# Part of the last expert's weights loaded early, first gather in four pieces, two chunks' keys interleaved at the start, in a hybrid decoder step

## The reference, cut to what matters

```python
m = rmsnorm(mem, g_mem); k = m @ w_k; v = m @ w_v                  # 256 memory tokens
x = x + mixer(rmsnorm(x, g_mix), ...)                              # w_in 1024x2560, w_out
x = x + cross_attn(rmsnorm(x, g_xattn), k, v, w_q, w_xo)           # 4 heads of 256; own cached k, v per sample
h = rmsnorm(x, g_moe)
top_logit, top_e = top_k(h @ w_router + b_router, 4)               # of 32 experts
gates = softmax(top_logit)
for each expert e:                                                 # tokens that chose e
    gate, up = split(x_e @ w1[e] + b1[e])                          # 1024 x 2048
    out_e = ((clip(up) + 1) * glu(min(gate, 7))) @ w2[e] + b2[e]   # 1024 x 1024
x = x + sum_e gate_e * out_e
y = rmsnorm(x, g_final)
```

## Time and profile before

| | |
|---|---|
| median of 3 runs | 1196.09 us (1193.36 to 1196.84) |
| the profiled execution | 1195.74 us |
| its span, first to last instruction | 1193.9 us |
| PE busy | 1157.0 us, 97% |
| DVE, ACT, POOL busy | 306.9, 157.7, 28.2 us |
| DMA | 458.34 MB, mean 384 GB/s |
| chain that ended last | PE 72%, DMA 25%, DVE 1%, ACT 1% |
| expert units of 2048 KB issued | 182, some 33 us from issue to landing |
| granted clock | 0.997 of full speed |

### The profile page before, as it was taken

One profiled execution on the slowest core, in us unless ns is written; L12 is line 12 of the kernel. 1 busy time (PEld: TensorE's weight loads), 2 busy tenths in 40 slices (PEclk: granted clock), 3 DMA queues, 4 the chain that ended last, 5 costly groups with the idle time before them and its releaser, 6 DMA issues.

```text
span 1193.9 us, 14908 instructions
## 1 busy us (share of the span) xinstructions
PE 1157.0 (97%) x5937; PEld 604.6 (51%) x5937; DVE 306.9 (26%) x638; ACT 157.7 (13%) x242; POOL 28.2 (2%) x63
## 2 busy tenths in 40 slices
PE   9999999999999999999999999999999999999997
PEld 8888888784434344444444343434343434343433
DVE  5124533332121212122222212121212121212124
ACT  2011011031101210121021011101110111010102
POOL 0000000000000000000000000000000000000000
PEclk9999999999999999999999999999999999999999
DMA  9963444998999999999999999999999999999995
GB/s 366 398 238 129 131 155 150 427 390 335 426 426 428 428 428 429 428 428 430 428 429 427 429 429 429 428 428 429 428 429 428 428 430 428 430 427 428 428 428 221
DMA packets 40398, 458.34 MB, mean 384 GB/s; under 512 B 6032, under 2 KB 6800, under 8 KB 8496
## 3 DMA queue, kind: packets, MB, share of 16 engines
q1 hardware_dynamic: 37440, 454.12, 90.7%
q10 hardware_dynamic: 2928, 3.80, 1.0%
HBM read 454.41 MB, written 3.23 MB: 383 GB/s over the span
## 4 chain that ended last, share of the span: by engine, by line
PE 72%; DMA 25%; DVE 1%; ACT 1%; issue 0%; SPq 0%; DVEq 0%; ACTq 0%
PE ps L1307 25%; PE ps L1084 15%; DMA ring<-in_w_dn 14%; PE ps L1425 13%; DMA arena<-in_w_dn 8%; PE ps L1281 7%; PE ps L1298 3%; DMA ring<-in_w_gu 3%; PE ps L1111 2%; PE ps L1318 2%; PE ps L1192 1%; DMA ring<-in_w_k 1%; PE ps L1177 1%; PE ps L1211 1%; PE ps L1167 1%; PE ps L1414 1%
## 5 line engine op out<-in xcount | busy, mean ns | idle before, releaser
L1307 PE MATMUL ps<-ring,arena 128*64 128x512 f32 x1536 | 349.9, 597 | 5.6 <-DMA ring<-in_w_gu 4.8
L1307 PEld LDWEIGHTS ps<-ring,arena 128*64 128x64 f32 x1536 | 103.1, 136 | 200.6 <-issue 184.7
L1084 PE MATMUL ps<-arena,ring 128*128 128x264 f32 (+1 forms) x800 | 178.9, 385 | 0.0
L1425 PE MATMUL ps<-ring,arena 128*64 128x512 f32 x736 | 165.4, 595 | 9.4 <-DMA ring<-in_w_dn 9.4
L1084 PEld LDWEIGHTS ps<-arena,ring 128*128 128x128 f32 x800 | 151.8, 190 | 25.3 <-issue 0.2
L1307 PE MATMUL ps<-arena 128*64 128x512 f32 x512 | 116.9, 598 | 2.8 <-DMA arena<-in_w_gu 2.4
L1020 DVE COPY arena<-ps 64x512 f32<-64x512 f32 x31 | 21.5, 694 | 369.1 <-PE ps L1425 369.1
L1425 PEld LDWEIGHTS ps<-ring,arena 128*64 128x64 f32 x736 | 52.7, 137 | 112.9 <-issue 106.8
L962 DVE TENSOR_TENSOR resid<-resid,ps 128x264 f32<-128x264 f32 x128 | 53.1, 429 | 173.3 <-PE ps L1298 172.8
L1281 PEld LDWEIGHTS ps<-arena 128*128 128x128 f32 x768 | 90.1, 195 | 14.8 <-issue 14.8
L1281 PE MATMUL ps<-arena 128*128 128x128 f32 x768 | 94.5, 280 | 1.8 <-ACT arena L626 1.8
(11 more groups left out here) (201 smaller groups left out, 504.4 us busy)
## 6 DMA issues: line engine op xcount, KB each, us to landing
ring<-in_w_gu SPq DMA_DIRECT2D x92, 2048.0 KB, 32.6
ring<-in_w_dn SPq DMA_DIRECT2D x44, 2048.0 KB, 32.9
arena<-in_w_gu SPq DMA_DIRECT2D x32, 2048.0 KB, 33.7
arena<-in_w_dn SPq DMA_DIRECT2D x14, 2048.0 KB, 32.8
ring<-in_w_in SPq DMA_DIRECT2D x10, 1024.0 KB, 27.5
ring<-in_kc SPq DMA_DIRECT2D x8, 1024.0 KB, 4.8
ring<-in_vc SPq DMA_DIRECT2D x8, 1024.0 KB, 5.1
ring<-in_w_gu SPq DMA_DIRECT2D x8, 1024.0 KB, 8.8
```

The costliest lines, as they stand in the source:

```text
L1084: last = mm(b[:, 0:width], w[:, k, P * (m % 2):P * (m % 2) + P], source(k), start=(k == 0), stop=(k == KT - 1))
L1307: last = mm(ps[64 * h:64 * h + 64, bank + n, :], tile[:, k, SLOTS * half:SLOTS * half + SLOTS], w[:, at:at + 512], start=(k == 0), stop=(k ...
L1425: last = mm(ps[64 * h:64 * h + 64, 4, :], hid[i % 2][:, k, :], w[:, at:at + 512], start=(k == 0), stop=(k == KT - 1))
```

## The change

Five edits stand in the diff.

1. **Start.** `FIRST_PARTS` has two parts left. After them comes the first half (k 0-3) of the second key chunk, then the second half of the memory, then the second halves of both key chunks. PE does m = 2, 3 for k 0-3 before m = 0 to 3 for k 4-7.
2. **Cross-attention.** DVE copies the probabilities of heads 0 and 1 before the sample softmax's reciprocal and scale. The copies have a semaphore of their own, `probs_copied`.
3. **Router and first gather.** The permutation moves from ACT's copies to the place where PE writes the transposes in PSUM: neighbouring columns of a transpose's output lie 128 floats apart. ACT reads and writes whole rows. `h_tok[2]` is not zeroed; the gather contracts over its 8 rows alone. The gather is issued quarter by quarter: only ga0 ahead of the first expert matmul, ga1 to ga3 in the middle of units 0, 1 and 2; the gates' transposes go to unit 3.
4. **Order in the experts' rounds.** For odd i: `gather_half` after u = 0, `turn_gate_up` after u = 1, `combine_two` after u = 2 and u = 3. In the last round but one the last expert's `turn_gate_up` goes into the down matmuls of expert 30, after two of their eight k.
5. **Stash.** The 1 MB row k = 7 of expert 31's gate and up is loaded to a buffer of its own in `arena` ahead of the kc chunks. Unit 3 of expert 31 then loads only its other 1 MB, and SP's step for it is split accordingly.

```diff
-FIRST_PARTS = [(0, 2), (2, 4), (4, 8)]
+FIRST_PARTS = [(0, 2), (2, 4)]
+ARENA = 23280
...
+        stash = view(stash_at, SLOT)
...
+            half = 256 * KT // 2
+            sp.dma_start(ring[:, 1, 0:half], w_k[1, :, 0:half]).then_inc(part_landed[2], 16)
+            sp.dma_start(mem_raw[:, KT // 2:, :], mem_t[:, KT // 2:, :]).then_inc(mem_in[2], 16)
+            for n in range(2):
+                sp.dma_start(ring[:, n, half:], w_k[n, :, half:]).then_inc(landed[n], 16)
...
+                if (kind, c) == ("kc", 0):
+                    rows = w_gu[NE - 1, KT - 2:KT].rearrange("k p n -> (k p) n")
+                    sp.dma_start(stash[:], rows.rearrange("(p j) n -> p (j n)", j=ROWS_GU)[:, SLOT:2 * SLOT]).then_inc(stash_in, 16)
...
+            last_step = turns * 4 + 2
+            unit_free(last_step, 3)
+            sp.dma_start(unit_buffer(n)[:, 0:SLOT],
+                         rows.rearrange("(p j) n -> p (j n)", j=ROWS_GU)[:, 0:SLOT]).then_inc(unit_landed[n], 16)
+            step(last_step, 2, NE - 2, NE - 1, range(4, UNITS))
...
-                by_row = h_tok[n // 2][0:rows, 512 * (n % 2):512 * (n % 2) + 512].rearrange(
-                    "t (b j p) -> t b p j", b=2, j=ROWS_GU)
-                nc.scalar.activation(by_row, bank(("htok", n))[0:rows].rearrange("t (b p j) -> t b p j", b=2, j=ROWS_GU),
+                nc.scalar.activation(h_tok[n // 2][0:rows, 512 * (n % 2):512 * (n % 2) + 512], bank(("htok", n))[0:rows],
                                      ACT.Copy, scale=rstd_tok[0:rows, n // 2:n // 2 + 1]).then_inc(tok_copied, 1)
...
+            for h in range(2):
+                copy_probs(h)
             dve.wait_ge(s_exp, 5)
             link(nc.vector.reciprocal(att_s[:, 8:9], att_s[:, 8:9]))
-            TS(s_s[:], s_s[:], att_s[:, 8:9], None, ALU.mult).then_inc(emptied, 1)
-            dve.wait_ge(kv_stored, 32)
-            for h in range(HEADS):
-                copy(probs_t[:, h, :, :], filled(("pT", h)).rearrange("p (m q) -> p m q", m=2)).then_inc(emptied, 1)
+            TS(s_s[:], s_s[:], att_s[:, 8:9], None, ALU.mult).then_inc(emptied, 1 + HEADS)
+            for h in range(2, HEADS):
+                copy_probs(h)
...
+            for m in range(2, 4):
+                keys(m, 0, KT // 2)
+            for m in range(4):
+                if m % 2 == 0:
+                    pe.wait_ge(landed[m // 2], 16)
+                keys(m, KT // 2, KT).then_inc(grp, 1)
...
-                    last = turn(b[0:width, P * f:P * f + P],
+                    pair = b[0:width, 2 * P * (f // 2):2 * P * (f // 2) + 2 * P]
+                    by_row = pair.rearrange("t (j h i) -> t h i j", j=ROWS_GU, h=2)[:, f % 2]
+                    last = turn(by_row,
                                 h_fm[:, 4 * (n % 2) + f, P * (n // 2):P * (n // 2) + width], ident[:])
...
-            gather(begin(("ga", 0)), 0, range(2), begun=True).then_inc(ga_filled, 1)
-            gather(begin(("ga", 1)), 0, range(2, 4)).then_inc(ga_filled, 1)
+            def gather_quarter(n):
+                return gather(begin(("ga", n)), n // 2, range(2 * (n % 2), 2 * (n % 2) + 2), begun=(n == 0))
+
+            gather_quarter(0).then_inc(ga_filled, 1)
...
+                pe.wait_ge(ga_copied, u + 1)
                 pe.wait_ge(unit_landed[u], 16)
                 halves = gate_up_unit(unit_buffer(u), u, xg[0], 0, FIRST_BANK)
                 next(halves).then_inc(half_used, 1)
-                if u == 1:
+                if u < 3:
+                    gather_quarter(u + 1).then_inc(ga_filled, 1)
+                else:
                     turn_gates()
...
+                            if i % 2:
+                                if u == 0:
+                                    gather_half()
+                                elif u == 1:
+                                    turn_gate_up(e)
+                                else:
+                                    combine_two(e, i, 2 * u - 4)
+                            elif u == 0:
                                 turn_gate_up(e)
...
-                    if early:
-                        turn_gate_up(e + 1)
...
+                            if early and k == 2:
+                                turn_gate_up(e + 1)
```

More of the change, by code:

```diff
@@ L234, in build @@
         unit_landed = [sem(f"unit_landed{n}") for n in range(RING_UNITS)]
-        part_landed = [sem(f"part_landed{n}") for n in range(2)]
+        part_landed = [sem(f"part_landed{n}") for n in range(3)]
         bias_split = sem("bias_split")
@@ L397, in unit_free, with step @@
                     sp.wait_ge(w_used, e * 4 + n - 2)
-            def step(e, i, expert, next_expert):
-                for n in range(UNITS):
+            def step(e, i, expert, next_expert, units=range(UNITS)):
+                for n in units:
                     unit_free(e, n)
@@ L436, in _ @@
             for i in range(3):
-                step(NE - 4 + i, i, NE - 4 + i, NE - 3 + i)
+                step(NE - 4 + i, i, NE - 4 + i, NE - 3 + i, range(UNITS if i < 2 else 3))
             sp.wait_ge(iters_ready, 2)
@@ L443, in _ @@
                 with sp.Fori(1, end >> 3) as again:
+                    step(again * NE - 2, 2, NE - 2, NE - 1, range(3, UNITS))
                     step(again * NE - 1, 3, NE - 1, 0)
@@ L448, in _ @@
                     for i in range(3):
-                        step(again * NE + NE - 4 + i, i, NE - 4 + i, NE - 3 + i)
+                        step(again * NE + NE - 4 + i, i, NE - 4 + i, NE - 3 + i, range(UNITS if i < 2 else 3))
+            last_step = turns * 4 + 2
+            unit_free(last_step, 3)
+            n = (STEP_AT[2] + 3) % RING_UNITS
+            rows = w_gu[NE - 1, KT - 2:KT].rearrange("k p n -> (k p) n")
+            sp.dma_start(unit_buffer(n)[:, 0:SLOT],
+                         rows.rearrange("(p j) n -> p (j n)", j=ROWS_GU)[:, 0:SLOT]).then_inc(unit_landed[n], 16)
+            step(last_step, 2, NE - 2, NE - 1, range(4, UNITS))
             for part, (k, k_end) in enumerate(LAST_PARTS):
@@ L656, in four_experts @@
                         pos = pos + 1
+                    if i % 2 and not final or i == 1:
+                        act.wait_ge(side_filled, pos + 2)
+                        copy_gathered(nxt, 1)
                     if not (final and i == 3):
@@ L1090, in _, with keys @@
             keep_busy(ps[:, 7, :], 9)
-            first_keys = ring[:, 0, :].rearrange("p (k n) -> p k n", k=KT)
+            first_keys = ring[:, 0:2, :].rearrange("p c (k n) -> p c k n", k=KT)
+            def keys(m, k_first, k_end):
+                for k in range(k_first, k_end):
+                    pe.wait_ge(mem_ready, k + 1)
+                    last = mm(bank(("k", m))[:, 0:NMEM], first_keys[:, m // 2, k, P * (m % 2):P * (m % 2) + P],
+                              mem[:, k, :], start=(k == 0), stop=(k == KT - 1))
+                return last
             for part, (k_first, k_end) in enumerate(FIRST_PARTS):
-                pe.wait_ge(landed[0] if part == 2 else part_landed[part], 16)
+                pe.wait_ge(part_landed[part], 16)
                 for m in range(2):
[L1095 to L1102, removed]
+                    keys(m, k_first, k_end)
+            pe.wait_ge(part_landed[2], 16)
+            for m in range(2, 4):
[4 more added lines that the diff above has]
+                keys(m, KT // 2, KT).then_inc(grp, 1)
                 if m == 2:
@@ L1105, in _ @@
                     sum_squares("mem_ssq", 1, NMEM, 2)
+            for m in range(4, KT):
+                project("w_k", m, lambda k: mem[:, k, :], "k")
             for c in range(4):
@@ L1280, in gather @@
                             pe.wait_ge(p_built if t == 2 else first_p, 1 if t == 2 else t + 1)
[L1281 removed]
+                        rows = P if t < 2 else NS
+                        last = mm(b[:, P * at:P * at + P], h_tok[t][0:rows, first:first + P], p_hot[0:rows, t, :],
                                   start=(t == 0), stop=(t == TT - 1))
                 return last
[L1285 removed]
+            pe.wait_ge(late_zero, 2)
             pe.wait_ge(tok_copied, 6)
[L1287 to L1288 removed]
+            def gather_quarter(n):
+                return gather(begin(("ga", n)), n // 2, range(2 * (n % 2), 2 * (n % 2) + 2), begun=(n == 0))
+            gather_quarter(0).then_inc(ga_filled, 1)
             pe.wait_ge(iters_ready, 2)
@@ L1386, in four_experts @@
                                 pe.wait_ge(side_copied, twin * 3 + 3 + u // 2)
-                            first, last = gate_up_unit(unit(u), u, xg[((i + 1) // 2) % 2], (i + 1) % 2)
+                            kept = None
+                            if early and u == 3:
+                                pe.wait_ge(stash_in, 16)
+                                kept = stash
+                            first, last = gate_up_unit(unit(u), u, xg[((i + 1) // 2) % 2], (i + 1) % 2, second=kept)
                             if i == 0:
```

63 lines of the change are left out of this document (28 added, 35 removed).

## The result

The changed kernel takes 1211.47 us (median of 4 runs, 1210.36 to 1213.26) against 1195.73 (4 runs by now); the ratio is 1.0136, 95% interval 1.0116 to 1.0156. It is slower by 15.7 us, outside the range, and on the other side. Its profiled execution spans 1211.4 us, 17.5 more than before.

A forecast was written before the change was run, and what follows sets the result against it. The end was taken as the weight stream's restart, its bytes and a fixed PE tail; 0.7 + 0.7 + 2.6 + 1.0 = 5.0 us off 1195.74 gave 1190.7, 1191.1 beside the median; own range 1189.2 to 1192.6, full range 1188.8 to 1195.2.

The forecast's parts named there:

- cost nothing while the stream binds: Experts' odd rounds: the new order's extra PE time stays hidden behind the weight stream; without this cover 5 us.
- Start: First key chunks: the 8 new matmuls cover PE's wait for the keys' third part; gain 0.7 us, bounds 0 and 1.1.
- Cross-attention: Before `attend`: DVE's first copy, moved ahead of the sample softmax, removes PE's wait; gain 0.7 us, bounds 0 and 0.7.
- Router and restart: Router and first gather: SP issues the first piece 3.7 us earlier, of which 2.6 stay; bounds 0.7 and 3.7.
- the first rival: Router transposes slower by a factor of two, the gather 2.7 us later; gain 2.3, time 1193.8 us; chance 0.17.
- the fourth: Router transposes cost far more than double, from a factor of 4 slower by over 0.3%, 1199.7 us; chance 0.06.
- the second rival: First quarters and half units: the clock still falls to 1.2 GHz, 1.5 us paid again, time 1192.6; chance 0.10.
- Tail: Last expert's transposes: ACT's copy covered by expert 30's down matmuls; gain 1.0 us, which the stash lets be had.
- Order of the rounds: Experts' odd rounds: parting gather and transposes costs PE 0.35 us for two experts, 55.5 against the stream's 58.8.
- The one for "slower": Router's 24 transposes: each further 0.12 us of one costs 2.9; a factor of 2.7 eats the gain; chance 0.06.
- a sign of being wrong: In the trace after: the transposes stretch, or the restart moves and PE's last DMA wait, at 1139.99, does not.

The follow-up runs named there:

- e1: The changed kernel with the gather's third matmul contracting over all 128 rows again; 1191.41 us, ratio 0.9966 to the kernel before.
- e3: The changed kernel with the three matmuls reversed in every second part of a gather, so two 8-row ones stand side by side; 1194.7 us, ratio 0.9995.
- e8: e1 with PE's two register loads of the iteration counts moved from ahead of the first half unit to behind unit 1; 1190.19 us, ratio 0.9958.
- e6: e1 with the old order of the odd rounds, transposes and gather both after u = 0; 1190.89 us, ratio 0.9967.

## Why the prediction was wrong

**What failed: edit 3's narrow matmul had no term.** The prediction described the edit ("the gather contracts over its 8 rows alone" stood in the list of the change, though its line is not among those of the diff shown there) and priced the copies, the order of the quarters, the clock and the transposes' output, but not this. Silently it was taken as free, and as belonging to the first gather. It is in `gather`, which all 32 gathers use. Measured: 8 changes of size a gather, 7 of them at 0.19 us, 1.34 us each gather, 2.7 us for two experts, some 43 us in all 32.

The trace of before had a row of this kind. L1362 transposes three tiles, the last with 8 rows; here it is on PE's timeline of the kernel before, with the start of the first round:

```profile
287.68 0.59 PE L1362 MATMUL ps<-ident,arena 128*128 128x128 f32 x3
288.20 3.65 PE L1307 MATMUL ps<-ring,arena 128*64 128x512 f32 x16
```

The three take 0.52 from start to start, where eight of L1318, all of one size, take 1.16, that is 0.44 for three at the same spacing. So three with a narrow one among them were 0.08 longer and not shorter. This row gives under half of the price that was measured, but it could have put the term on the list: seven such changes in 32 gathers are 18 us.

**Second failure: "cost nothing while the stream binds" was not turned into the right number.** It stood for the order of the rounds, with the cover as 55.5 against the stream's 58.8, 3.3 us for two experts, as if the whole part were bound by the stream. But PE starts the rounds some 25 us behind the stream (an estimate: it gains 3.6 us for two experts and takes from 288 to 675, 7 double rounds, to catch up) and has to make this up first. 662.51, where the prediction has PE begin to wait, is the start of a transfer in the chain; PE's own first wait for a weight is at 674.96. What can be hidden is only what PE loses to the stream behind that. From the first round to the last down unit of expert 29 the kernel before took 1143.57 - 288.20 = 855.4 us, of which 15 by 55.16, less the 0.52 of one L1362, so 826.9, is work: 28.5 lost to the stream, 1.9 for two experts. (PE's list of waits has 21.6 of them.) Above some 57.1 PE binds everywhere. Three kernels mark this line: e1 at 55.53 is at its full gain, e3 at 57.07 has one DMA piece left in its chain, the changed kernel at 58.21 has none.

This closes the account. From 289.62 to 1162.30 the changed kernel takes 872.7, 15 by 58.21 less 0.5, so 17.3 more than before; it enters the rounds 1.4 later, and its tail is 1.2 shorter; together 17.5, the difference of the spans. The narrow matmuls are 15 by 2.68 of the 17.3 and the new order 15 by 0.37, together 45.8, less the 28.5. So in the changed kernel the new order was not hidden: its 5.5 us counted in full.

**The other terms, point by point**, from e1, which holds all of the change but the narrow matmul. There the predicted 1191.1 stands against 1191.41. That they agree so well is partly luck: against the span before, e1's is 5.7 us shorter, of which the start is 1.7 (0.7 predicted), the attention 0.95 (0.7), the router 1.8 (2.6) and the tail 1.2 (1.0), so the errors cancel.

- *Start, 0.7.* In the seven other traces that have this edit, the first w_v matmuls (L1111 before, L1145 in e1) start at 33.64 to 34.69, against 35.48 and 35.32 in the two without it: a gain of 0.6 to 1.8, in four of them above the stated bound of 1.1. In the profiled execution of the changed kernel it was nothing, the lower bound that was given: the new piece landed only at 10.3.
- *Cross-attention, 0.7.* `attend` came 0.9 earlier, w_xo 0.96 with the same start. Right, somewhat low.
- *Router and restart, 3.7 at the issue and 2.6 at the end.* In e1 the issue comes at 266.31, 5.85 earlier; 1.7 and 0.95 of that came with the start and the attention, 3.2 are this edit's. Unpriced were the register loads (0.8, e8): PE stood 1.38 us ahead of the first half unit, where 0.7 was taken for the copy. At the last wait for expert 29 (1139.99 before, 1135.52 in e1) 4.5 are left, so 1.8 of this edit. The step was right, and its size at the end too high by 0.8. The transposes cost nothing extra, 2.38 us for twenty in every trace: the first rival, and the fourth with it, is out. The Trainium skill's sentence on non-contiguous PSUM patterns (Advanced Engine Details and Errata, Memory Cachelines) does not hold for these twenty: 2.38 us with outputs 128 floats apart and without.
- *The clock.* In the changed kernel it did fall to 0.50, behind a gap of 0.96 us, and the first half unit took 3.61 in place of e1's 1.94, 1.7 more, about the 1.5 of the second rival. In e1 it stayed at 1.00, behind a gap of 1.38. Of the eight traces with this edit it fell in one, which does not speak against the chance of 0.10; what decides is open.
- *Tail, 1.0, with the stash.* Right: 53.9 before, 52.7 in e1, 53.6 without the stash, 54.0 without the moved transposes.
- *Order of the rounds, 0.35 for two experts, hidden.* 55.53 - 55.16 = 0.37; hidden as long as the narrow matmul is out (e6), and not hidden with it.

The rivals missed it for the same reason as the sum. The one for "slower" looked for its cost in 24 transposes; the cost was in 256 changes of size, 8 in each of 32 gathers. What was announced as a sign of being wrong did show it at once: the restart moved, and the last DMA wait did not merely stay, it was gone.

## What to carry to other kernels

List every operand shape that an edit alters, and multiply each by the number of times that the line runs, before looking at the places that the edit was made for. A helper used once at a critical spot and thirty times elsewhere is priced by the thirty. When a cost is said to be hidden behind another engine, work out the cover as the waits that are left (here 28.5 us in 15 double rounds, 1.9 each), not as the difference of the two rates: beyond that sum the bound changes sides, and each further microsecond counts in full.

## What the runs showed of the hardware

- In a row of 128-column matmuls, changing the number of rows that they contract over, from 128 to 8 or to 64, or back, costs 0.19 us at each change: 4.22 us for a gather with 7 such changes inside it and 3.65 with 4, against 2.88 with none; 4.23 with 64 rows. The single record is only 21 ns longer. Leaving out rows that are known to be zero made the gather slower by nearly half. A change of size that falls on the step from the gather to the experts' matmuls costs nothing: the step is 200 ns with it and 205 without.
- Transposes that write neighbouring float32 columns 128 floats apart in PSUM took the same 2.38 us for twenty as contiguous ones. ACT's copies of a half tile, freed of their permutation, went from 0.95 to 0.6 us apart, and a single one from between 1.09 and 1.18 us to between 0.66 and 0.69.
- Two register loads on PE held back the matmul behind them: in e1 it started 0.85 us after the copy that it needed was done, and 0.06 after it with the loads moved away (e8).
- The granted clock was 0.50 behind a gap of 0.96 us in one execution and 1.00 behind one of 1.38 in another.
